# Ten more dense tiles loaded behind the norms, 58 dots left to the picks, and row gathers placed between one-hots

## What is computed

```
s1, s2 = query . sub_keys_1, query . sub_keys_2      # 8 heads, 128 keys each
top 16 of each, then top 16 of the 256 sums          # 128 experts per token, of 16384
gate   = softmax(top)
act    = gelu(einsum('td,tkd->tk', h, expert_u[idx]))
out    = einsum('tk,tkd->td', gate * act, expert_v[idx])
```

## Time and profile before

| what | us |
|---|---|
| median of 3 runs | 2042.28 (2040.76 to 2043.44) |
| the profiled execution's own time | 2040.3 |
| its span in the trace | 2038.6 |
| queries (L1193), to the start of the tile stage | 803 to 925 |
| tile stage | 925.3 to 1312.2 |
| picks | 1312 to 1491 |
| second block | 1491 to 1529 |
| v stage and ending | 1529 to 2038.6 |

### The profile page before, as it was taken

The page is one execution under the profiler, slowest core; times in us unless marked ns, Lnnn a source line. Parts: engine busy times, 40 slices in busy tenths (PEclk is TensorE's granted clock), DMA queues, the critical chain, the costliest instruction groups (busy, mean ns, idle before and its releaser), DMA issues.

```text
span 2038.6 us, 24582 instructions
## 1 busy us (share of the span) xinstructions
PE 1881.9 (92%) x8897; PEld 1437.0 (70%) x8897; DVE 1350.9 (66%) x2603; ACT 420.0 (21%) x848; POOL 770.0 (38%) x803
## 2 busy tenths in 40 slices
PE   3899999999999899999999999978989999999980
PEld 3788888888888546888888888867874444444430
DVE  6845556556566403379888886699976665666678
ACT  2022222222222102001111111377850000000000
POOL 2012321322232100146443334336885544544455
PEclk8789999999999999999999999999999999999995
DMA  9936546645754666199999999987619999999998
GB/s 395 421 146 253 205 174 253 227 153 210 268 192 167 239 232 227 55 379 357 409 409 407 405 406 408 391 244 227 196 63 380 409 409 410 409 409 409 410 385 303
DMA packets 140451, 614.15 MB, mean 301 GB/s; under 512 B 15536, under 2 KB 15664, under 8 KB 117040
## 3 DMA queue, kind: packets, MB, share of 16 engines
q1 hardware_dynamic: 66192, 325.09, 41.2%
q0 software_dynamic: 73728, 285.25, 36.9%
q10 hardware_dynamic: 416, 2.25, 0.3%
HBM read 608.33 MB, written 4.19 MB: 300 GB/s over the span
## 4 chain that ended last, share of the span: by engine, by line
PE 62%; DMA 20%; DVE 11%; POOL 4%; issue 2%; ACT 1%; DVEq 0%; ACTq 0%
PE ps L1283 19%; DMA arena<-in_v_rows,arena 18%; PE ps L969 15%; PE ps L1193 5%; PE ps L1017 5%; PE ps L1052 4%; POOL arena L569 3%; DVE arena L1788 2%; DVE arena L1411 2%; DVE arena L1719 2%; DVE ps L1727 2%; PE ps L1338 2%; PE ps L1057 2%; DMA arena<-in_ada 1%; PE ps L1309 1%
## 5 line engine op out<-in xcount | busy, mean ns | idle before, releaser
L1368 PE MATMUL ps<-arena 128*128 128x512 f32 x1024 | 441.9, 595 | 5.2 <-DMA arena<-in_v_dense 4.6
L1788 DVE SCALAR_TENSOR_TENSOR arena<-arena 128x1024 f32<-128x1024 f32 x254 | 326.3, 1285 | 170.8 <-DMA arena<-in_v_rows,arena 166.3
L569 POOL DMA_INDIRECT arena<-in_u_rows,arena x256 | 259.0, 1012 | 352.9 <-DVE arena L1719 293.2
L1283 PE MATMUL ps<-arena 128*128 128x256 f32 x1792 | 386.9, 379 | 0.0
L1368 PEld LDWEIGHTS ps<-arena 128*128 128x128 f32 x1024 | 201.7, 197 | 244.1 <-issue 237.8
L1283 PEld LDWEIGHTS ps<-arena 128*128 128x128 f32 x1792 | 341.0, 190 | 45.7
L569 POOL DMA_INDIRECT arena<-in_v_rows,arena x256 | 262.1, 1024 | 238.9 <-DVE arena L1788 215.6
L969 PE MATMUL ps<-arena 128*128 128x256 f32 x1440 | 339.3, 380 | 0.0
L1719 DVE SCALAR_TENSOR_TENSOR arena<-arena,ps 128x1152 f32<-128x1152 f32 x208 | 279.0, 1350 | 62.8 <-DMA arena<-in_u_rows,arena 62.5
L969 PEld LDWEIGHTS ps<-arena 128*128 128x128 f32 x1440 | 262.5, 191 | 29.1
L1390 DVE SCALAR_TENSOR_TENSOR arena<-arena 128x2048 f32<-128x2048 f32 x60 | 142.8, 2380 | 0.0
(11 more groups left out here) (268 smaller groups left out, 2054.3 us busy)
## 6 DMA issues: line engine op xcount, KB each, us to landing
arena<-in_ada SPq DMA_DIRECT2D x96, 1024.0 KB, 5.1
arena<-in_v_dense SPq DMA_DIRECT2D x128, 512.0 KB, 6.8
arena<-in_u_dense SPq DMA_DIRECT2D x128, 448.0 KB, 6.9
arena<-in_w_in SPq DMA_DIRECT2D x45, 1024.0 KB, 6.8
arena<-in_w_tail SPq DMA_DIRECT2D x32, 1024.0 KB, 7.0
arena<-in_w_in SPq DMA_DIRECT2D x12, 512.0 KB, 16.6
arena<-in_u_rows,arena POOLq DMA_INDIRECT x256, 11.3
arena<-in_v_rows,arena POOLq DMA_INDIRECT x256, 10.4
```

The source lines that it names most:

```text
L569: nc.gpsimd.indirect_dma_start(out=row, out_offset=None, in_=table[:, :], in_offset=bass.IndirectOffsetOnAxis(ap=i32(idx[:, b, k:k + 1]), ...
L1283: last = mm(bank(5 + j % 2, 0, T), u_tile[j % len(u_tile)][:, k, :], h2T[:, k, :], start=(k == 0), stop=(k == KU - 1))
L1368: last = mm(sums(b)[:, lo:hi], dense[:, b, j // 2, :, j % 2], w[:, lo:hi], start=(j == 0), stop=(j == NKEYS - 1))
L1788: stt(total[b], row, w, total[b], ALU.mult, ALU.add).then_inc(v_sum, 1)
```

## The change

Three things move. Ten more buffers for dense u tiles are laid over memory that is free at that time, and tiles 4 to 13 are loaded into them right behind the norms. LATE goes from 192 to 198, and six of the quarters from q = 32 on (37, 42, 47, 53, 58, 63) do no dot. WEIGH_AT goes from LATE + 40 = 232 to LATE + 35 = 233, and of the six v gathers that stood before the second block's one-hots four are placed between them.

```diff
+        early_at = [junk_at + GU + n * KU * P for n in range(2)] + [q_at + KC * T + n * KU * P for n in range(2)] + [acc_at + n * KU * P for n in range(6)]
+        early_tile_u = [view(a, KU, P) for a in early_at]
...
+        def product_slot(j):
+            n, m = len(u_tile), len(early_tile_u)
+            if n <= j < n + m:
+                return early_tile_u[j - n], early_u_land[j - n], 1
+            i = j if j < n else j - m
+            return u_tile[i % n], tile_land[i % n], i // n + 1
...
             sp.dma_start(rows_of(out), xs[:, :, :]).then_inc(stored, 16)
+            sp.wait_ge(a2.sem, a2.at("exp1"))
+            for j in range(4, 8):
+                product_tile(j)
+            sp.wait_ge(mod_sum, 7)
+            for j in range(8, 10):
+                product_tile(j)
+            sp.wait_ge(v2.sem, v2.at("xn11"))
+            sp.wait_ge(stored, 16)
+            for j in range(10, 4 + len(early_tile_u)):
+                product_tile(j)
             for q in range(4, 10):
...
-            for j in range(4, NKEYS):
-                sp.wait_ge(tile_ps, j - 3)
+            for j in range(4 + len(early_tile_u), NKEYS):
+                sp.wait_ge(tile_ps, j - 3 if j >= 8 + len(early_tile_u) else j - 3 - len(early_tile_u))
                 product_tile(j)
...
                 gather(v_row[n % len(v_row)], v_rows, b, k, v_land[n % len(v_row)])
-                if n == len(v_row) - 1:
-                    for q in range(P // 4, T // 4):
+                if 0 < n < len(v_row):
+                    for q in range(P // 4 + 6 * (n - 1), P // 4 + 6 * n if n < len(v_row) - 1 else T // 4):
                         weigh(q)
...
-                dots(ndot[0], ndot[0] + 1)
-                ndot[0] += 1
+                if q < P // 4 or q % 16 not in (5, 10, 15):
+                    dots(ndot[0], ndot[0] + 1)
+                    ndot[0] += 1
...
-LATE = TB * KTOP - 64
+LATE = TB * KTOP - 58
-WEIGH_AT = LATE + 40
+WEIGH_AT = LATE + 35
```

More of the change, by code:

```diff
@@ L243, in build_layer @@
         u_tile = [view(a, KU, P) for a in tile_at]
+        early_at = [junk_at + GU + n * KU * P for n in range(2)] + [q_at + KC * T + n * KU * P for n in range(2)] + [acc_at + n * KU * P for n in range(6)]
+        assert early_at[1] + KU * P <= q_at and early_at[3] + KU * P <= arena_size - D and early_at[9] + KU * P <= half_at[1] - D
+        early_tile_u = [view(a, KU, P) for a in early_at]
         gate, idx1f, idx2f = (view(front_at + n * TB * KTOP, TB, KTOP) for n in range(3))
@@ L316, in build_layer @@
         tile_land = [sem(f"u_tile_landed{s}") for s in range(len(u_tile))]
+        early_u_land = [sem(f"early_u_tile_landed{s}") for s in range(len(early_tile_u))]
+        v_tile_land = [sem(f"v_tile_landed{s}") for s in range(len(v_tile))]
         tile_ps, tile_out = sem("u_tile_product"), sem("u_tile_evacuated")
@@ L417, in product_tile @@
             def product_tile(j):
-                sp.dma_start(u_tile[j % len(u_tile)].rearrange("p a b -> p (a b)"), u_dense[j]).then_inc(tile_land[j % len(u_tile)], 16)
+                dst, landed, _ = product_slot(j)
+                sp.dma_start(dst.rearrange("p a b -> p (a b)"), u_dense[j]).then_inc(landed, 16)
             sp.wait_ge(w_used, WOUT + 16)
@@ L440, in _ @@
                     sp.wait_ge(u_dot, last_use(UROWS - 1))
-                sp.dma_start(v_tile[j % len(u_tile)], v_dense[j - NKEYS]).then_inc(tile_land[j % len(u_tile)], 16)
+                sp.dma_start(v_tile[j % len(v_tile)], v_dense[j - NKEYS]).then_inc(v_tile_land[j % len(v_tile)], 16)
                 if j - 4 == NKEYS + (TB + 1) * D // P:
@@ L1278, in _ @@
             for j in range(NKEYS):
-                pe.wait_ge(tile_land[j % len(u_tile)], 16 * (j // len(u_tile) + 1))
+                w, landed, count = product_slot(j)
+                pe.wait_ge(landed, 16 * count)
                 if j >= 2:
@@ L1282, in _ @@
                 for k in range(KU):
-                    last = mm(bank(5 + j % 2, 0, T), u_tile[j % len(u_tile)][:, k, :], h2T[:, k, :], start=(k == 0), stop=(k == KU - 1))
+                    last = mm(bank(5 + j % 2, 0, T), w[:, k, :], h2T[:, k, :], start=(k == 0), stop=(k == KU - 1))
                 last.then_inc(tile_ps, 1)
@@ L1362, in _ @@
             for j in range(NKEYS):
-                s = (NKEYS + j) % len(u_tile)
-                pe.wait_ge(tile_land[s], 16 * ((NKEYS + j) // len(u_tile) + 1))
-                w = v_tile[s]
+                w = v_tile[j % len(v_tile)]
+                pe.wait_ge(v_tile_land[j % len(v_tile)], 16 * (j // len(v_tile) + 1))
                 for b in range(TB):
```

## The result

| | before | after |
|---|---|---|
| median, us | 2041.70 (2038.44 to 2043.44, 10 runs) | 2047.59 (2044.31 to 2051.36, 10 runs) |
| ratio of the two | | 1.0032, 95% interval 1.0024 to 1.0040 |
| profiled execution; its span | 2040.3; 2038.6 | 2047.2; 2045.5 |

A forecast was written before the change was run, and what follows sets the result against it. TensorE without idle time in the tile stage and DMA full in the v stage left everything decided between 1307 and 1529 us. Terms 3.9 + 4.1 - 3.3 - 5.0 + 3.0 - 1.7 = +1.0 us gave 2043.3 us, range 2036 to 2049.

The forecast's parts named there:

- No change: Whole kernel: time within 0.2% (4.1 us) of before, median 2043.3 us; chance 0.45.
- three signs that I had named for an error: VectorE finds row 234 landed; first pick not later; v stage changes in length by more than 1 us.
- Term 5: Second block: four v gathers between its one-hots cost +3.0 us, bounds 2.2 to 4.8.
- Term 6: Start of second block: TensorE's clock no longer falls after 2 us of idleness, -1.7 us, bounds -2 to 0.
- The loads, and what they free: Tile stage: ten loads cost nothing in a DMA hole; VectorE gains 3.3 us in about 940 to 972 us.
- Term 1: End of tile stage: six more dots before the picks delay the first pick by +3.9 us, bounds 0 and +7.
- Term 2: First one-hot: row 234 comes late at q = 36, one stall of +4.1 us, bounds 0 to 5.
- Term 3: Second half of the picks: six fewer dots save 0.4 in five quarters, 1.27 in the last; -3.3 us.
- Term 4: Ahead of the second block: two v gathers for six, four fewer at 1.24 us each, -5.0 us.
- The rival with GpSimd and the low clock as this block's bound: Second block: each of four gathers shows 1.2 us, TensorE keeps low clock; +1.8 + 1.7 = 2046.8 us; chance 12%.

The follow-up runs named there:

- experiment 3: Kernel before with the ten early loads alone (LATE 192, all dots, v gathers as before): ratio 1.0001, 2040.82 us.
- experiment 11: Kernel of experiment 1, but VectorE makes all four weighted one-hots of a first-block quarter and GpSimd none: ratio 1.0042, 2048.46 us.
- experiment 1: Changed kernel with GpSimd's lead of five rows given back; no gather in quarters without a dot: ratio to the kernel before 1.0005, 2041.71 us.
- experiment 7: Kernel of experiment 6 with the six v gathers one by one between the first block's last one-hots: ratio to the kernel before 0.9960, 2032.72 us.
- Experiment 8: Changed kernel with 32 unread identity matmuls on TensorE ahead of the first token_weights: ratio to the kernel before 1.0028, 2047.29 us.
- experiment 6: Changed kernel with the six dotless quarters at the end (q = 58 to 63) and the lead of five rows: ratio to the kernel before 0.9983, 2036.50 us.
- 4: Changed kernel without the spread, all six v gathers ahead of the second block's one-hots: ratio to the kernel before 1.0035, 2047.95 us.
- experiment 2: Kernel before with only the spread: four v gathers between the second block's one-hots: ratio 0.9993, 2038.75 us.
- experiment 10: Kernel before with only its six v gathers moved, one by one ahead of first-block one-hots (w = 24 to 29): ratio 0.9973, 2035.26 us.
- 9: Kernel of experiment 7 with LATE 195, three dotless quarters at the end, v gathers ahead of w = 21 to 26: ratio to before 0.9949, 2030.38 us.
- 12: Kernel of experiment 9 without the ten early loads: ratio to the kernel before 0.9958, 2031.98 us.
- experiment 5: Kernel before with LATE 198, the same six dotless quarters and the lead of five rows, without early loads: ratio 1.0039, 2048.64 us.

## Why the prediction was right in its places and wrong in its sum

The forecast was 2043.3 us, no change, by terms that sum to +1.0; measured is +6.5. The range of 2036 to 2049 took the median in, by its width more than by its terms: three of the ten executions lie above it. "No change" had the largest chance, 0.45; what came had 0.28. None of the three signs that I had named for an error came up: row 234 was missed, the first pick was late, the v stage kept its length. The places were right and the prices of two of them weren't; what follows the first pick had no term at all.

In the trace, against the forecast, term by term: the first pick +2.1 us for +3.9; from there to q = 36 +2.1 for nothing; the stall +6.1 for +4.1; the missing dots -0.7 (+0.4 and -1.1) for -3.3; the wait ahead of the second block -4.9 for -5.0; the block itself +3.6 for +1.3 (terms 5 and 6); the v stage +0.5 for nothing; and 1.95 less for the tile stage's earlier end.

- **The loads, and what they free: right.** 3.25 us gained (experiment 3) for 3.3 forecast, and nothing beyond.
- **Term 1 (+3.9): mis-sized.** 6 x 1.42 - 6.66 = 1.9 us is what the six dots cost when rows come in time, and 2.05 was measured. Of the 2.0 us more in the forecast, 0.8 were for the v tiles' loads; some 1.3 came from turning the 3.3 us gained into 1.4 rows and these back into 2.0 us, where experiment 3 shows the whole 3.25 us at the first pick. The 2.05 is also one draw of a wide spread: with the same code up to the first pick it stood 0.7, 0.8, 2.1, 2.8, 3.2, 3.8 and 4.9 us later than before (experiments 11 and 1, the changed kernel, 7, 8, 6 and 4). Late rows do it (0.62 us in one, 1.52 in another); without the loads it is 7.4, the upper bound given. What I left out is that the lateness goes on behind the first pick: +2.1 us up to q = 36, 0.5 of it further waits for rows in the first quarters, 1.2 at q = 32 to 34 where TensorE's clock came down to 0.50. Why it fell there, ahead of any missing row, stays open. It did so in experiments 6 and 11 too; in the kernel before it didn't, though TensorE stood 1.48 and 1.56 us there as against 1.48 and 1.26, nor in experiment 1, whose code is that of experiment 11 up to there.
- **Term 2 (+4.1): the wait was right, its consequence missed.** VectorE waited 3.71 us. But the three quarters took 6.1 us more, and this is the step that failed: I charged the clock's fall to the idleness ahead of the second block only, and not to the new idleness that the stall itself makes. TensorE stood 4.90 us, ran at half clock, and VectorE waited 2.84 us for it. Experiment 8 holds the clock and shortens q = 37 and 38 by 1.4 us in all; by it the clock's share is 1.0 to 2.4 us, where the stall cost 2.0 more than forecast. Experiment 1 takes the late row away and with it 4.6 of the 6.1 us (10.06 us for 14.68); by the ratios it is 5.5 us faster.
- **Term 3 (-3.3): failed.** In the second half of the picks, only the last quarter's dot was saved (part of the -6.0 in the table; 4.9 of that is term 4). A quarter without a dot lasts 2.61 us, a gain of 0.25 for the 0.4 that I took, and three or four of the next four last 2.98 for 2.86. The one-hots of the earlier trace rows's quarter in the kernel before, then those of such a quarter in the kernel after:

```profile
1446.15 1.63 POOL L585 TENSOR_SCALAR arena<-arena 128x128 f32<-128x128 f32 x2
1446.51 0.59 DVE L1772 TENSOR_SCALAR arena<-arena 128x128 f32<-128x128 f32 x2
1428.66 1.75 POOL L610 TENSOR_SCALAR arena<-arena 128x128 f32<-128x128 f32 x2
1429.20 0.79 DVE L1797 TENSOR_SCALAR arena<-arena 128x128 f32<-128x128 f32 x2
```

  VectorE's pair takes 0.79 us for 0.59 and GpSimd's 1.75 for 1.63. GpSimd's own round before is 0.17 + 1.03 + 0.03 + 1.63 = 2.86 us, with nothing left over: it was as full as VectorE, and I had looked only at VectorE and TensorE. That the missing dots shift the two against each other until they overlap badly is my reading and not shown; when GpSimd's pair began 0.54 us ahead, VectorE's took 0.79 us in the kernel after and 0.59 in experiment 2. A missing dot isn't needed for it either. Quarters 59 to 62 of the kernel before last 2.98 to 3.00 us, as do 53 to 57 of experiment 6 (2.98 to 3.09): quarters with a dot, in which GpSimd has one-hots and no gather left. With a v gather in each of the last four, experiment 10 has them at 2.86 to 2.90; experiment 7, with v gathers in q = 54 to 57, at 2.92 to 2.97. What sets the longer rhythm stays open; that it costs 0.12 us a quarter is shown.
- **Term 4 (-5.0): right**, 7.07 to 2.14 us, 4.93.
- **Term 5 (+3.0): inside its bounds**, 3.5 by experiment 2. (The lower bound of 2.2 doesn't follow from the term's parts; they give 0.3 + 3 x (1.2 - 0.42) = 2.6.) The rival with GpSimd and the low clock as this block's bound (2046.8) had 1.8 us more for the gathers and 1.7 for the clock; 0.5 and 1.6 of these came.
- **Term 6 (-1.7): not in this kernel.** With 2.10 to 2.18 us of idleness ahead of the block the clock held in two kernels (experiments 2 and 6) and fell in three (the changed kernel, experiments 1 and 8), at about 1.6 us each time. I had counted it whole in the sum, with no row to say so; its bounds held both outcomes. With 0.3 us (7, 9 and 12) it held each time, behind 7.1 us (before, 3, 4 and 5) it fell each time.

Put together: experiments 1 to 3 and 5 say the parts' worth against before, each with 2 to 3 us of uncertainty: loads alone 0; spread alone -1.4; dots with the lead, without loads, +8.0; all three with the lead +1.0; without the lead +6.5. The loads are worth something only together with six dots whose rows would otherwise be late, and six dots missing here and there among the quarters weren't worth moving.

For the stretched one-hots the rows of experiment 11 give the sign and a size: 0.23 us for one gather's start beside four of them, and nothing for another. The Trainium skill ("SBUF — State Buffer", section on the two separate sides) describes the port pair that VectorE, in a mode that uses two ports, shares with GpSimd as an exclusive lock, where the one that comes second is blocked for the other's whole instruction. If VectorE's one-hots are such work, one that meets a gather of 0.94 us would by that stand for most of it; the rows show a quarter of that at most. And in the earlier trace rows's quarter VectorE's pair took its 0.59 us wholly inside GpSimd's 1.63, for 0.55 alone (1.10 for four). So the rule in this form doesn't fit here. Which part of an instruction has to meet which part of the other stays open.

## What to carry to other kernels

When a wait is added in a loop whose engines are all nearly full, add to its length what the stall does to TensorE's clock; and before work is taken from one engine, count the round of every other engine in the loop, including the one that only issues gathers. A lead of rows that looks like slack (five gathers) was what covered the one late row. Of three parts that were changed at once, the one with a gain (gathers of the next stage issued where GpSimd has a free slot already) was worth some 5 us when placed right (experiment 7 against 6, and 10) and 1.4 us as it was, the latter not clear of noise.

## What the runs showed of the hardware that was not expected

- TensorE's granted clock fell to the lower level behind 2.1 us of idleness ahead of the second block in three kernels and not in two others, and behind 1.45 us in experiment 10, so a forecast has to carry it as a chance, not as a yes or no. At 0.50 to 0.58, eight matmuls of `token_weights` took 2.05 us for 1.13.
- The same two one-hots of VectorE took 0.59, 0.79 or 1.04 us (experiment 5) beside GpSimd's work, and GpSimd's pair 1.57 to 1.76 us; four took 1.10 us alone and 1.33 with one gather's start in them.
- Rows' lateness at the end of the tile stage scatters by 4 us between executions of the same instructions, which is as much as a whole term of the forecast.
